# Attention 0 of a diffusion trunk: which engine copies the outputs out of their PSUM banks

## The reference, cut to what matters

```python
def one_block(qi):
    s = jnp.einsum('bqhmd,bkhmd->bhmqk', qi, k) * scale          # two score maps for each head
    p = jnp.einsum('bhmqk,m->bhqk', jax.nn.softmax(s, axis=-1), w)   # w = (1, -lambda)
    return jnp.einsum('bhqk,bkhd->bqhd', p, v)
...
o = rmsnorm(blocked_attention(maps(q), k, v, map_w, scale), subln_g) * (1 - lam_init)
```

## Time and profile before

| what | us |
|---|---|
| median of 3 runs (lowest, highest) | 1907.77 (1907.06, 1908.58) |
| the profiled execution, its own time | 1904.45 |
| its span in the trace | 1902.6 |
| TensorE busy in the span | 1825.9 |
| VectorE busy | 1263.2 |
| ScalarE busy | 1075.0 |
| attention 0, from its first scores to its last copy | 175.5 to 220.6 |

### The profile page before, as it was taken

One profiled execution on the slowest core, in us unless ns is written; L12 is line 12 of the kernel. 1 busy time (PEld: TensorE's weight loads), 2 busy tenths in 40 slices (PEclk: granted clock), 3 DMA queues, 4 the chain that ended last, 5 costly groups with the idle time before them and its releaser, 6 DMA issues.

```text
span 1902.6 us, 23200 instructions
## 1 busy us (share of the span) xinstructions
PE 1825.9 (96%) x9612; PEld 1481.5 (78%) x9612; DVE 1263.2 (66%) x1186; ACT 1075.0 (57%) x1098; POOL 25.8 (1%) x27
## 2 busy tenths in 40 slices
PE   6998898999999989978999999999999999999997
PEld 4876576888888867647888888888888888888886
DVE  4344626232233273283888989889898898988987
ACT  5333535222232254364777777777777777777775
POOL 0000000000000001020000000000000000000000
PEclk9998999999999999999899999999999999999999
DMA  9653254623223262342799999999999999999994
GB/s 336 188 179 109 84 160 140 193 89 111 89 93 107 89 216 78 100 133 103 268 374 374 356 381 331 367 373 368 370 339 366 374 365 372 338 378 373 365 376 160
DMA packets 263217, 473.89 MB, mean 249 GB/s; under 512 B 16121, under 2 KB 115377, under 8 KB 263105
## 3 DMA queue, kind: packets, MB, share of 16 engines
q1 hardware_dynamic: 262720, 471.38, 70.0%
q0 software_dynamic: 384, 0.95, 0.2%
HBM read 471.25 MB, written 1.05 MB: 248 GB/s over the span
## 4 chain that ended last, share of the span: by engine, by line
PE 90%; DVE 4%; ACT 2%; DMA 1%; issue 1%; SPq 1%; POOL 0%; DVEq 0%; ACTq 0%
PE bank L542 27%; PE bank L544 27%; PE bank L543 27%; PE bank L609 1%; PE bank L2166 1%; PE bank L2129 1%; PE bank L399 1%; DMA raw_weights<-in_ev_w_in 1%; PE bank L811 1%; SPq L1083 1%; PE bank L412 1%; ACT split_high L521 1%; PE bank L893 0%; DVE small L961 0%; DVE y L872 0%
## 5 line engine op out<-in xcount | busy, mean ns | idle before, releaser
L1669 DVE TENSOR_TENSOR split_low<-raw_weights,split_high 128x2048 fp32r<-128x2048 f32 x224 | 512.8, 2289 | 42.5 <-ACT split_high L1418 41.6
L1418 ACT ACTIVATE split_high<-raw_weights 128x2048 fp32r<-128x2048 f32 x222 | 426.0, 1919 | 139.5 <-PE bank L544 139.5
L526 DVE TENSOR_TENSOR split_low<-raw_weights,split_high 128x1024 fp32r<-128x1024 f32 x118 | 144.1, 1227 | 293.6 <-ACT split_high L521 293.6
L542 PE MATMUL bank<-h_high,split_high 128*128 128x512 f32 (+1 forms) x832 | 317.5, 382 | 8.8 <-DVE h_low L456 5.2
L543 PE MATMUL bank<-h_low,split_high 128*128 128x512 f32 (+1 forms) x832 | 314.3, 378 | 0.0
L544 PE MATMUL bank<-h_high,split_low 128*128 128x512 f32 (+1 forms) x832 | 314.2, 378 | 0.0
L1669 DVE TENSOR_TENSOR h_low<-raw_weights,h_high 128x2048 fp32r<-128x2048 f32 x112 | 256.7, 2292 | 54.5 <-ACT h_high L1418 53.4
L542 PE MATMUL bank<-split_high,xe_high 128*128 128x512 f32 x672 | 266.3, 396 | 0.0
L544 PE MATMUL bank<-split_high,xe_low 128*128 128x512 f32 x672 | 262.2, 390 | 0.0
L543 PE MATMUL bank<-split_low,xe_high 128*128 128x512 f32 x672 | 261.9, 390 | 0.0
L1418 ACT ACTIVATE h_high<-raw_weights 128x2048 fp32r<-128x2048 f32 x112 | 215.0, 1920 | 50.2 <-PE bank L544 50.2
(11 more groups left out here) (281 smaller groups left out, 2435.7 us busy)
## 6 DMA issues: line engine op xcount, KB each, us to landing
raw_weights<-in_moe_w SPq DMA_DIRECT2D x336, 1024.0 KB, 6.9
raw_weights<-in_w_mod SPq DMA_DIRECT2D x48, 1024.0 KB, 7.2
raw_weights<-in_ffn_w SPq DMA_DIRECT2D x33, 1024.0 KB, 5.4
raw_weights<-in_ev_w_in SPq DMA_DIRECT2D x10, 1024.0 KB, 10.2
raw_weights<-in_od_w_in SPq DMA_DIRECT2D x8, 1024.0 KB, 7.4
raw_weights<-in_ev_w_out SPq DMA_DIRECT2D x4, 1024.0 KB, 9.2
raw_weights<-in_od_w_out SPq DMA_DIRECT2D x4, 1024.0 KB, 9.2
overlay<-in_rpb SPq DMA_DIRECT2D x32, 64.0 KB, 2.4
```

Source lines behind the costliest of these rows:

```text
L526: dve.tensor_tensor(half_of(s, j, SPL[:, s % NSPLIT, :]), half_of(s, j, raw_of(split_at[s])), half_of(s, j, SPH[:, s % NSPLIT, :]).bitcast ...
L542: pe.matmul(ps, wh, xh, start=first, stop=False)
L1418: act.activation(esplit(u)[0], RAW[:, u % NRAW, :], ACT.Copy).then_inc(S("e_high"), 1)
L1669: dve.tensor_tensor(lo, RAW[:, u % NRAW, :], hi.bitcast(F32), ALU.subtract).then_inc(S("e_low"), 1)
```

## The change

The VectorE copies are taken out of `dve_attention`, whose loop shrinks from 19 to 17 steps; `act_attention` gets the same eight copies as ScalarE activations, behind its other work of the steps i = 4, 6, ..., 18, with the same semaphores.

```diff
@@ act_attention, at the end of step i
                        .then_inc(S(f"pt{a}"), 1)
+                if i >= 4 and i % 2 == 0:
+                    p = (i - 4) // 2
+                    src, dst = pair_out(units, p)
+                    act.wait_ge(S("o0"), p + 1)
+                    act.activation(OUN[dst], src, ACT.Copy).then_inc(S("o_evac0"), 1)
 
         def dve_attention(dve, a, units, between=lambda i: None):
-            lag = 3 + a
-            for i in range(len(units) + lag):
+            for i in range(len(units) + 1):
                 between(i)
...
-                if i >= lag and (i - lag) % 2 == 1:
-                    p = (i - lag) // 2
-                    src, dst = pair_out(units, p)
-                    dve.wait_ge(S("o0"), p + 1)
-                    dve.tensor_copy(OUN[dst], src).then_inc(S("o_evac0"), 1)
```

## The result

The changed kernel takes 1910.05 us (median of 22 runs, 1908.26 to 1915.16), the kernel before, run beside it, 1907.45 us (22 runs, 1904.14 to 1910.87). The ratio is 1.0017 with a 95% interval from 1.0010 to 1.0024, so the change costs 3.2 us (1.9 to 4.6). That is "no change" by the bound of 0.2%, but a loss that can be told from zero, and larger than the forecast of 1.2.

The account below looks back on a forecast made before the run. TensorE, busy for 96% of the span, was taken to bound the kernel. Loop gain -0.14 plus tail +1.34 gave +1.20 us, from 1907.77 to 1909.0; the 8-in-10 range was 1906.8 to 1911.6.

Parts of the forecast that it names:

- The loop's gain: Attention 0 loop: three reductions on VectorE start earlier without the copies ahead of them, 0.14 us together.
- ScalarE's copies in the loop: Attention 0 loop: each new copy holds ScalarE 0.28 us but costs 0; rival up to 1.7 us more, chance 0.04.
- both covers: ScalarE in the loop: slack 0.95 us behind copies of pairs 0, 2, 4 and idle 0.58 behind 1, 3, 5.
- The tail: End of attention 0: the table load queues behind the last ScalarE copy, so the squares come 1.34 us later.
- the longer way: A possibility given chance 0.02; its description is not in the text given.
- The shift reaches the end: Behind attention 0: the DMA wait for `w_mod` gives no cover, so the 1.34 us delay carries through rigidly.
- The clock stays: TensorE ahead of the sums: idle time grows from 0.96 to 2.30 us without a clock fall, so no cost.
- the prediction's own sign: TensorE behind the sums: a clock under 1.00 between 222 and 236 us would show the forecast wrong.
- the rival's bounds: Clock fall behind the widened gap ahead of the sums: 1.8 to 5.0 us lost, chance 0.10.
- The row that I leaned on: TensorE in the profile of before: a 2.19 us gap ahead of 215.16 left the clock at 1.00.
- the clock's case: Rival: TensorE's clock falls behind the widened gap ahead of the sums; shift +3.0 to +6.2 us, chance 0.10.
- The likeliest case: Whole kernel: +1.20 us, giving 1909.0 us, with chance 0.77.

Follow-up runs that it names:

- after_again: The changed kernel once more, unchanged, for a second profile; median 1910.05 us.
- only_last: The kernel before with only the last of the eight copies moved to ScalarE; median 1910.17 us.
- before_load_behind: The kernel before, all copies on VectorE, but ScalarE waits for the last with a tiny one-column copy ahead of the table load; ratio 1.0009.
- before: The first profile of the kernel before, without any change; median of its runs 1907.45 us.
- after: The first profile of the changed kernel, all eight copies on ScalarE; median of its runs 1910.05 us.
- before_third: The kernel before, unchanged, profiled a third time; no time is given under this name.
- last_on_vector: The changed kernel with the last copy left on VectorE, the other seven on ScalarE; median 1908.86 us.
- table_ahead: The changed kernel with ScalarE's small square root and its table load put ahead of the wait for the last product; ratio 1.0012.
- before_table_late: The kernel before, with ScalarE waiting for VectorE's last copy directly ahead of its small square root; ratio 1.0006.
- after_filled_two: The changed kernel with two needless TensorE products between its last product and the sums; ratio 1.0013.
- after_filled: The changed kernel with four needless TensorE products between its last product and the sums; no whole time is given.

## Why the prediction was right, and where not

- *The loop's gain, -0.14.* Right: -0.12 from the first scores to the transposes at the loop's end (39.67 to 39.55). The whole loop is 1.24 us longer in this pair only because the low clock at its end added 1.36. The reductions of units 5 and 9 start at 187.92 and 197.62 in the changed kernel, so a head takes 9.70 us; before it was 188.20 and 197.94, 9.74. The three positions show an idle time of 0.20 where the copy was, and the scores are what is late next, as forecast.
- *ScalarE's copies in the loop, 0.* Right: 0.27 us each where 0.28 was forecast, and both covers held.
- *The tail, +1.34.* Right: squares 1.85 us behind the product's end (forecast 1.84), sums 2.51 (forecast 2.52), +1.33 against before. From load to small activation it was 1.29 us, from that to the squares 0.12, and from the copy's end to the load 0.02. The squares began 1.41 us behind the load's start, and 1.40 or 1.41 in `after_again`, `only_last` and `before_load_behind`: no run shows the longer way to which the prediction gave 0.02.
- *The shift reaches the end.* Right as far as the projection, and in the pair of `before` and `after` to the end: TensorE's wait for the `w_mod` buffer was 1.10 us before and 1.03 after, so it hid nothing, and the remainder of the span behind the projection was equal to 0.2 us. Over other profiles it isn't shown, as the remainder moves by more than the shift.
- *The clock stays.* This step failed. By the prediction's own sign (a clock under 1.00 between 222 and 236 us: it was 0.63 from 224 to 228) the forecast was wrong in its mechanism. The forecast argued that the new idle time of 2.30 us was hardly longer than one of 2.19 that had left the clock at 1.00, and gave a fall 0.10. In the profiles it fell behind the sums in four of the four with the widened idle time, in none of the seven with the old one, and in none of the three where needless products filled it. The prediction's low times (10.0 and 3.6 us) are divided by 0.5: 0.50 is what the trace of before shows from 174 to 182 us and from 242 to 244. The fall's price was 1.6 us, a little under the lower end (1.8) that the rival's bounds gave. The row that I leaned on was a poor witness: other profiles of the same kernel show a fall behind that very idle time of 2.19 us (`before_third`: 0.50 from 216 to 218 us).
- *The sum.* -0.14 + 1.33 + 1.6 = 2.8 us, 1910.2 from the median of 1907.45; measured 1910.05, and 3.2 (1.9 to 4.6) by the ratio. This agreement proves little, as kernels without these terms came out 1.3 and 2.3 us over before (`last_on_vector`, `table_ahead`). The forecast of "no change" and the range (up to 1911.6) held because the range had been stretched to the lower end of the clock's case, and because the clock's price came out a little under that end: that was luck. The likeliest case, +1.20, was too low by the one term, which it had put at nothing.

Open: whether ScalarE's copies make the low clock at the loop's end more frequent; how much of the spread of the remainder behind the projection (1661.6 to 1666.2 us) comes from the kernel, as the unchanged one alone covers 2.2 us of it; whether a part of the 2.9 us is given back there; and with it the 2 us by which some kernels with the tail of before, the unchanged one among them, lie over the pooled runs of before. The times alone show neither the 1.33 nor the 1.6 us by itself.

## What to carry to other kernels

Before moving a cheap instruction to another engine, read what is queued behind it there: here 0.38 us of copy were free, but its wait pushed a 1.28 us table load from under a product onto the path. A table switch belongs ahead of the wait that ends a stage (with it there, in `table_ahead`, the squares came 0.46 us behind the product instead of 1.85). And when a change widens an idle time of TensorE that is followed by dense work, price the clock as part of the sum (here 1.6 us beside 1.33), and don't take one profile's unbroken clock behind a similar gap as proof that it will hold.

## What the runs showed of the hardware that I had not expected

- In `before_table_late` the wait for VectorE's last copy stands ahead of the small square root, and the table load that comes with this root did not wait: it ran at 218.88, the root at 221.41, 2.5 us later. Where ScalarE had a waiting instruction of its own ahead of them, the load came behind that: the tiny copy at 222.86 and the load at 223.07 in `before_load_behind`, the last copy at 221.15 and the load at 221.55 in the changed kernel.
- TensorE was granted 0.50 of its clock for some 3.6 us (an estimate from the clock missing between 220 and 240 us, 0.91 granted: 0.09 x 20/0.5) behind the idle time of 2.29 to 2.55 us ahead of the sums in the four profiles that had it unfilled (`after`, `after_again`, `only_last`, `before_load_behind`), though it had worked for the 2 us ahead of it; with two products in this idle time (1.88 us, `after_filled_two`) the clock stayed at 1.00. The fall came not at once but 1.1 to 1.9 us into the sums (in the changed kernel 1.6: the third group, at 225.20, is the first at 0.66), so the work that paid is not the work that waited.
- Four fp32 products of 128 rows and 512 columns took 3.60 us (`after_filled`), 0.90 each. The two of 64 rows and 512 columns in a unit's scores took 1.13 together, and not one behind the other: in the trace of the kernel before, a record of each starts at 192.00 (0.69 us) and again at 192.54 (0.59), under 0.01 us apart. My price for the needless products had halved the 1.13.
- The ratio of the unchanged kernel to itself was 1.0012 with 11 runs beside 28, and 0.9999 with 12 beside 35. Nothing under 0.1% should be read from one such ratio.
